# Low-rank outputs of a recurrence: two 64-row products on the two row halves of the array in place of two zero-padded 128-row products

## The chip, the core and the metric

The kernel runs on one core of a Trainium2 chip. The metric is the device time of one execution in microseconds (us), median of the runs. Engines are named as in the profile: PE is TensorE's matmul side, PEld its weight load, DVE VectorE, ACT ScalarE, POOL GpSimd, SP the engine that issues most of the DMAs.

## The reference, cut to what matters

The program is a whole network block (feed-forward, an RWKV-7 recurrence beside dilated attention, feed-forward) followed by two layers of another block. The change lies in the preparation of the recurrence. D_MODEL and RWKV_WIDTH are 1024, SEQ is 256, DECAY_LORA and AAA_LORA are 64, GATE_LORA is 160:

```python
p = token_shift(p, mu)
r, k, v, wd, ad, gd = _split_last(p, (RWKV_WIDTH, RWKV_WIDTH, RWKV_WIDTH,
                                      DECAY_LORA, AAA_LORA, GATE_LORA))
w = -jax.nn.softplus(-(w0 + jnp.tanh(wd) @ w2)) - 0.5     # w2: 64 x 1024
decay = jnp.exp(-jnp.exp(w))
a = jax.nn.sigmoid(a0 + ad @ a2)                          # a2: 64 x 1024
g = jax.nn.sigmoid(gd) @ g2                               # g2: 160 x 1024
```

`tanh(wd) @ w2` (decay) and `ad @ a2` (the in-context learning rate) contract over 64 rows each, the gate over 160.

## The kernel before, in words

Activations lie transposed: channels on the 128 partitions, the 256 tokens along the free dimension. Each of the 8 output tiles (KT = 8) of a projection to 1024 channels is one PSUM bank region of 128 x 256. All operands are float32, and every `matmul` of the source shows as two weight-load records and two MATMUL records in the trace ("x64" in a row is 32 matmuls). All matmuls of the kernel go through one helper, line 1055.

Each engine's program is written out by hand in its order, and semaphores join them: PE counts finished tiles up in `tile_done`, ACT counts the tiles that it has read out of PSUM up in `act_out`, and PE waits for `act_out` before it writes a bank again. Work is divided into stages, in this order around the change:

1. `rwkv_lora_in`: 3 tiles of 8 matmuls; ACT copies each tile (line 2348), DVE blends it with the token before (lines 3175, 3177) into the slot `sBH` of `arena`. Slot tile 0 then holds wd on partitions 0 to 63 and ad on 64 to 127, tile 1 the first 128 rows of gd, tile 2 its last 32 rows on partitions 0 to 31. DVE has zeroed tile 2 whole (line 3161) and the upper half of tile 3 (line 3160) ahead of that.
2. `rwkv_k`: 8 tiles of 8 matmuls. Beside its first tiles ACT prepares the low-rank inputs (lines 2355 to 2359): it copies ad to tile 3, takes tanh of wd, writes zeros over ad in tile 0, takes the sigmoid of gd, and says `lora_ready`.
3. `rwkv_lora_out` (lines 1382 to 1399 on PE, 2362 to 2376 on ACT): the stage of the change. For each of 8 channel tiles j there are three PSUM tiles, numbered q = 3j + c and written to bank q % 4: c = 0 decay, c = 1 learning rate, c = 2 gate. The weight slab has w2 on partitions 0 to 63 and a2 on 64 to 127 of its first part, so both products of before use all 128 rows of that part, against tile 0 (wd over zeros) and against tile 3 (zeros over ad). The gate takes two accumulated matmuls. ACT reads each tile out (lines 2371, 2373, 2375), and ahead of tile q = 9 it takes a square over the whole key tensor (line 2366). PE waits ahead of tile q until tile q - 4 has been read out.
4. `head_sums`: 4 matmuls of 512 columns to banks 4 to 7; then `rwkv_r0` and so on, projections of 8 matmuls per tile to banks 0 to 3.

Of the kernel before, what the change touches and what calls it, by code (L numbers as in the profile page):

```python
# [15 lines left out]
ACT = mybir.ActivationFunctionType  # L16
AX = mybir.AxisListType

P = 128
D = 1024  # L20
KT = D // P
T = 256
# [3 lines left out]
SLAB = 32 * P  # L26
# [509 lines left out]
def program(nc, x_in, ctx_in, wide_in, down_in, par_in, const_in, const1_in, const2_in, out, dbg=None):  # L536
    with ExitStack() as ctx:
# [15 lines left out]
        S = {n: ctx.enter_context(nc.semaphore(n)) for n in sem_names}  # L553

        def sb(name, n):
            return ctx.enter_context(nc.sbuf_tensor(name, [P, n], F32))

        ring = sb("weights", SLOTS * SLAB)
# [12 lines left out]
        bank = [ctx.enter_context(nc.psum_tensor(f"bank{b}", [P, 512], F32)) for b in range(8)]  # L571
# [8 lines left out]
        def tiles(buf, base, n, width):  # L580
            return buf[:, base:base + n * width].rearrange("p (k t) -> p k t", k=n)
# [28 lines left out]
        def wtile(st, j, q, n=P):  # L610
            base = st.slot(j) * SLAB + q * P
            return ring[:, base:base + n]


        def slot(k):
            return A[:, k * HALF:(k + 1) * HALF]

        def slot3(k):
            return slot(k).rearrange("p (k t) -> p k t", k=KT)

        sR, sA, sB, sK, sBH, sKH, sV, sL, sAA, sG = range(10)
# [282 lines left out]
        def rows_gi_em(n):  # L904
            return (ROWS_GI, ROWS_EM)[n]
# [43 lines left out]
        def fn_folded(g, ns):  # L949

            low = ZF[:, 2 * g, 0:ns]
            odd_sums = A[:, 14336 + g * 2 * EVEN:14336 + g * 2 * EVEN + ns * EVEN].rearrange("p (s t) -> p s t", s=ns)
            return low[:, :, 0:EVEN], odd_sums, low[:, :, EVEN:T]
# [96 lines left out]
        def _(pe):  # L1050
            t = Tally(pe, S, None)
            mm = nc.tensor.matmul

            def matmul(out, lhsT, rhs, start=True, stop=True):
                return mm(out, lhsT, rhs, start=start, stop=stop, skip_group_check=True)  # L1055

            def transpose(out, in_):
                return nc.tensor.transpose(out, in_, ident[0:in_.shape[0], 0:in_.shape[0]])  # L1058
# [323 lines left out]
            st = ST["rwkv_lora_out"]  # L1382
            arrived(st, 0)
            t.wait("lora_ready")
            lora = tiles(A, sBH * HALF, 4, T)
            for j in range(KT):
                for c in range(3):
                    q = 3 * j + c
                    pe.wait_ge(S["act_out"], st.act0 + q - 3)
                    cols = ring[:, st.slot(0) * SLAB:st.slot(0) * SLAB + 3 * D].rearrange("p (a n) -> p a n", a=3)[:, :, j * P:(j + 1) * P]  # L1390
                    dst = bank[q % 4][:, 0:T]
                    if c == 0:
                        last = matmul(dst, cols[:, 0], lora[:, 0])
                    elif c == 1:
                        last = matmul(dst, cols[:, 0], lora[:, 3])
                    else:
                        matmul(dst, cols[:, 1], lora[:, 1], stop=False)
                        last = matmul(dst, cols[:, 2], lora[:, 2], start=False)
                    last.then_inc(S["tile_done"], 1)

            def head_sums(ready, src, done):

# [282 lines left out]
            st = ST["dil_qk"]  # L1685
            arrived(st, 2)
            for c in range(4):
                for k in range(KT):
                    last = matmul(bank[c][:, 0:T], wtile(st, 2, c * KT + k), H1[:, k], start=k == 0, stop=k == KT - 1)
# [9 lines left out]
            for q in range(2):  # L1699
                for k in range(12):  # L1700
                    n = 24 * q + 2 * k
                    last = matmul(bank[4][:, n:n + 2], sq[:, k, q * P:(q + 1) * P], pair[:, 0:P:64])
# [5 lines left out]
            for k in range(6):  # L1708
                for q in range(2):
                    n = 24 * q + 12 + 2 * k  # L1710
                    cols = (k % 2) * T + q * P
                    for g in range(2):
                        rows = slice(64 * g, 64 * g + 64)
                        last = matmul(bank[5 + k // 2][rows, cols:cols + P], DIL_R[:, n + g:n + g + 1].to_broadcast([P, 64]), ident)
# [67 lines left out]
            for q in range(2):  # L1782
                for b in range(2):
                    for c in range(3):
                        last = transpose(bank[4 + 2 * q + b][:, c * P:(c + 1) * P], y1[:, q, (3 * b + c) * P:(3 * b + c + 1) * P])
# [32 lines left out]
            for la in range(2):  # L1818
                nq = 2 * T if la == 0 else T
                p = f"l{la}_"  # L1820
# [37 lines left out]
                for n in range(2):  # L1858
                    for c in range(4):
                        last = transpose(bank[5 + n][:, c * P:(c + 1) * P], rows_gi_em(n)[:, c * P:(c + 1) * P])  # L1860
# [173 lines left out]
                for g in range(4):  # L2034
                    out = bank[4][32 * g:32 * g + 32, 0:ns * EVEN].rearrange("p (s t) -> p s t", s=ns)
                    last = matmul(out, DFT_EDGE, fn_folded(g, ns)[0])
                last.then_inc(S["pe_for_act"], 1)
                t.wait("fn_halves", 4)
                if la == 0:
# [26 lines left out]
                    last = FT // 2 - 1  # L2066
# [13 lines left out]
                else:  # L2080
# [16 lines left out]
                    for which in BLOCKS:  # L2097
                        half, q = int(which[0]) - 1, int(which[1]) - 1
                        turn_out(which, lambda i: bank[X_BANKS[2 * half + i // 2]][:, (i % 2) * T + q * P:(i % 2) * T + (q + 1) * P])
            out_sq = tiles(G, 0, KT, T)  # L2100
            for k in range(KT):
                t.wait("squares_ready")
                for q in range(2):
                    last = matmul(bank[1][:, 2 * q:2 * q + 2], out_sq[:, k, q * P:(q + 1) * P], ones[:, 0:2], start=k == 0 and q == 0, stop=k == KT - 1)
            last.then_inc(S["sums_ready"], 1)
            t.wait("rstd_ready")
            for q in range(2):
                last = matmul(bank[5][:, q * P:(q + 1) * P], RSTD[:, 2 * q:2 * q + 1].to_broadcast([P, P]), ident)
# [4 lines left out]
        def _(act):  # L2113
            t = Tally(act, S, "act_steps")
            af = nc.scalar.activation
# [236 lines left out]
            shift_in("k", 0)  # L2352
            act.wait_ge(S["shift_done"], 3)
            lora = tiles(A, sBH * HALF, 4, T)
            t.step(af(lora[64:128, 3], lora[64:128, 0], ACT.Copy))
            t.step(af(lora[0:64, 0], lora[0:64, 0], ACT.Tanh))
            t.step(af(lora[64:128, 0], lora[64:128, 0], ACT.Copy, scale=0.0))
            t.step(af(lora[:, 1], lora[:, 1], ACT.Sigmoid))
            t.out(af(lora[0:32, 2], lora[0:32, 2], ACT.Sigmoid), "lora_ready")
            for q in range(1, 8):  # L2360
# [1 line left out]
            st = ST["rwkv_lora_out"]  # L2362
            for q in range(24):
# [3 lines left out]
                j, c = q // 3, q % 3  # L2367
# [132 lines left out]
            for b in range(4):  # L2500
                t.wait("dve_for_act")
                cols = slot(sV)[:, b * 512:(b + 1) * 512]
# [6 lines left out]
            for n in range(14):  # L2509
# [15 lines left out]
                for tile in dil_filled(n):  # L2525
                    if tile >= 4:
                        st = ST["dil_gate0"]
# [37 lines left out]
            for la in range(2):  # L2565
                nq = 2 * T if la == 0 else T
                qtiles = nq // P
                p = f"l{la}_"
# [144 lines left out]
                if la == 0:  # L2713
# [22 lines left out]
                    st = ST[p + "ffn_up"]  # L2736
# [64 lines left out]
        def _(dve):  # L2801
            t = Tally(dve, S, "dve_steps")
# [354 lines left out]
            for k in range(KT):  # L3157
                t.out(stt(H1[:, k], columns[k], pc("mix_norm", k), r, mul, mul), "h_ready")
            shift = H[:, HALF:HALF + 4 * 257].rearrange("p (b n) -> p b n", b=4)
            t.step(nc.vector.memset(slot3(sBH)[0:64, 3], 0.0))  # L3160
            t.step(nc.vector.memset(slot3(sBH)[:, 2], 0.0))
            t.out(nc.vector.memset(shift[:, :, 0:1], 0.0), "dve_for_act")
            dif = H[:, HALF + 1040:HALF + 1296]
            n_shift = [0]
# [95 lines left out]
            for b in range(4):  # L3260
                c = slice(b * 512, (b + 1) * 512)
# [267 lines left out]
            for la in range(2):  # L3529
                nq = 2 * T if la == 0 else T  # L3530
                qtiles = nq // P
                p = f"l{la}_"
# [200 lines left out]
                for n in range(len(units) + 3):  # L3733
# [4 lines left out]
                    if n >= 3:  # L3738
                        h, q = units[n - 3]
# [66 lines left out]
                if la == 0:  # L3806
# [35 lines left out]
                    st = ST[p + "ffn_up"]  # L3842
# [59 lines left out]
                else:  # L3902
                    fn_gates = tiles(A, 16384, 4, 2 * T)
                    merge(p + "fn", G2, nq, False, halves=(fn_gates, fn_gates))
                    for j in range(2):
                        st = ST[p + "out"]
# [25 lines left out]
            for half in range(2):  # L3932
                dve.wait_ge(S["x_gained"], 4 * half + 4)
                rows = slice(4 * half, 4 * half + 4)
# [260 lines left out]
```

## Time and profile before

| | |
|---|---|
| median of 3 runs | 3098.05 us (3097.92 to 3098.75) |
| the profiled execution | 3097.39 us, span 3095.6 us |
| PE busy | 3022.0 us, 98% of the span |
| DVE, ACT, POOL busy | 1705.4, 600.4, 520.0 us |
| the stage of the change on PE | 259.16 to 273.86 us of the span |
| mean granted TensorE clock | 0.993 of full speed |

The span runs from the first to the last instruction; a time of the trace is counted from the span's start. In rows of a timeline a piece merges neighbouring instructions of one kind: its second figure runs from the first start to the last end, and since a matmul is pipelined (its end lies well behind the moment at which the next can start), how long a group occupied PE is read from its start to the start of the next group. "128*128" or "64*128" is the part of the array that is used (rows * columns), "128x256" the moving operand (partitions x columns).

### The profile page before, as it was taken

What the parts mean: (1) busy time and instruction counts of PE and PEld (TensorE: products, weight loads), DVE (VectorE), ACT (ScalarE), POOL (GpSimd) and SP (SyncE); (2) the same over time, 40 slices, a digit from 0 to 9 for tenths busy, and PEclk for the clock granted to TensorE, in tenths of its full rate; (3) what the DMA queues carried; (4) which work ended last, traced back from release to release, by engine and by line L of the source; (5) the groups of instructions that cost most, each with busy time, mean ns of one, the idle gap of its engine ahead of it and who ended that gap; (6) DMA issues with size and microseconds to landing.
All of it is one profiled execution on the core that took longest, in us unless ns stands there. A gap on an engine that the chain in (4) does not pass through costs nothing.

```text
span 3095.6 us, 37908 instructions
## 1 busy us (share of the span) xinstructions
PE 3022.0 (98%) x15542; PEld 2275.2 (74%) x15542; DVE 1705.4 (55%) x2518; ACT 600.4 (19%) x1186; POOL 520.0 (17%) x210
## 2 busy tenths in 40 slices
PE   8999999999999999999999999999999999999999
PEld 4448788775448857887588888888888888678544
DVE  6744642547766556666863358777424513722574
ACT  2104212222111112102611121110021201511111
POOL 4320000013332100221021212221110001000332
PEclk9999999999999999999999999999999999999999
DMA  5544411345553311442012234443232143133452
GB/s 222 207 171 167 187 57 33 133 151 176 194 190 109 123 41 63 148 136 95 28 68 82 82 143 143 155 142 137 97 116 93 64 160 112 55 150 129 153 189 109
DMA packets 54812, 388.14 MB, mean 125 GB/s; under 512 B 8816, under 2 KB 23152, under 8 KB 33776
## 3 DMA queue, kind: packets, MB, share of 16 engines
q1 hardware_dynamic: 50000, 380.48, 34.2%
q10 hardware_dynamic: 4640, 5.24, 0.8%
q8 instruction: 123, 2.02, 0.3%
q14 instruction: 49, 0.40, 0.0%
HBM read 371.79 MB, written 1.05 MB: 120 GB/s over the span
## 4 chain that ended last, share of the span: by engine, by line
PE 92%; DVE 5%; ACT 1%; issue 1%; DMA 0%; DVEq 0%; SPq 0%; ACTq 0%
PE bank L1055 91%; PE bank L1058 1%; DVE factors L3074 0%; DVE factors L2976 0%; DVE weights L3061 0%; DVE h_T L2858 0%; DVE small L3720 0%; DVE arena L3091 0%; DVE weights L3064 0%; DVE masks L3853 0%; DMA params<-params_dram 0%; ACT arena L2676 0%; DVE arena L3764 0%; ACT h_T L2164 0%; DVE arena L3675 0%
## 5 line engine op out<-in xcount | busy, mean ns | idle before, releaser
L1055 PE MATMUL bank<-h_T,weights 128*128 128x256 f32 (+1 forms) x3184 | 779.5, 397 | 16.3 <-ACT h_T L2164 4.0
L1055 PEld LDWEIGHTS bank<-h_T,weights 128*128 128x128 f32 x3184 | 598.9, 191 | 156.0 <-issue 69.3
L2785 POOL TENSOR_TENSOR weights<-weights 128x1024 f32<-128x1024 f32 (+2 forms) x103 | 264.3, 2566 | 1337.2 <-DMA weights<-wide_slabs_dram 1238.7
L2796 POOL TENSOR_TENSOR factors<-weights 128x1024 f32<-128x1024 f32 (+2 forms) x103 | 257.7, 2502 | 1206.7 <-PE bank L1055 1022.3
L1055 PE MATMUL bank<-arena,weights 128*128 128x256 f32 x1784 | 397.0, 381 | 4.9 <-DVE arena L3466 2.5
L1055 PEld LDWEIGHTS bank<-arena,weights 128*128 128x128 f32 x1784 | 339.6, 191 | 54.2 <-DVE arena L3466 2.7
L1055 PE MATMUL bank<-weights,h_T 128*128 128x256 f32 (+2 forms) x1040 | 339.6, 475 | 3.5 <-DMA weights<-wide_slabs_dram 2.2
L1055 PE MATMUL bank<-factors,weights 128*128 128x256 f32 x1432 | 323.9, 379 | 5.9 <-DVE arena L3091 4.3
L1055 PE MATMUL bank<-weights,factors 128*128 128x256 f32 (+1 forms) x936 | 304.1, 470 | 2.7 <-DVE weights L3061 1.5
L1055 PEld LDWEIGHTS bank<-factors,weights 128*128 128x128 f32 x1432 | 271.7, 190 | 44.2 <-DVE arena L3091 5.5
L1055 PEld LDWEIGHTS bank<-weights,h_T 128*128 128x128 f32 x1040 | 198.0, 191 | 127.1 <-issue 101.7
L3061 DVE TENSOR_TENSOR weights<-weights,factors 128x1024 f32<-128x1024 f32 (+2 forms) x103 | 127.4, 1237 | 266.0 <-PE bank L1055 240.5
L1055 PEld LDWEIGHTS bank<-weights,factors 128*128 128x128 f32 x936 | 178.8, 192 | 112.4 <-issue 93.3
L3064 DVE TENSOR_TENSOR weights<-weights,factors 128x1024 f32<-128x1024 f32 (+2 forms) x103 | 130.7, 1269 | 169.7 <-PE bank L1055 168.6
L2274 ACT ACTIVATE arena<-bank 128x512 f32<-128x512 f32 (+1 forms) x144 | 83.3, 580 | 695.3 <-PE bank L1055 622.9
L1055 PE MATMUL bank<-factors 128*128 128x256 f32 (+3 forms) x808 | 214.4, 411 | 0.0
L3091 DVE TENSOR_TENSOR arena<-bank,arena 128x512 f32<-128x512 f32 (+1 forms) x132 | 88.1, 667 | 194.7 <-PE bank L1055 192.0
L1055 PEld LDWEIGHTS bank<-factors 128*128 128x128 f32 (+1 forms) x808 | 150.9, 190 | 48.8 <-issue 31.8
L1055 PE MATMUL bank<-arena 64*64 64x64 f32 (+7 forms) x1544 | 174.0, 304 | 9.7 <-ACT arena L2676 6.4
L1055 PE MATMUL bank<-weights,arena 128*128 128x512 f32 x396 | 174.5, 593 | 3.3 <-DVE weights L3061 3.3
L1055 PEld LDWEIGHTS bank<-arena 64*64 64x64 f32 (+2 forms) x1544 | 122.2, 160 | 52.1 <-issue 24.8
L3853 DVE SCALAR_TENSOR_TENSOR masks<-arena 128x1024 f32<-128x1024 f32 x88 | 152.5, 1733 | 2.9
(367 smaller groups left out, 2662.1 us busy)
## 6 DMA issues: line engine op xcount, KB each, us to landing
weights<-wide_slabs_dram SPq DMA_DIRECT2D x147, 2048.0 KB, 7.8
arena<-wide_slabs_dram SPq DMA_DIRECT2D x61, 512.0 KB, 4.1
weights<-down_slabs_dram SPq DMA_DIRECT2D x8, 1408.0 KB, 6.1
merged_T<-arena SPq DMA_DIRECT2D x240, 32.0 KB, 1.9
merged_T<-wide_slabs_dram SPq DMA_DIRECT2D x15, 512.0 KB, 4.6
arena<-arena ACTq DMA_DIRECT2D x16, 256.0 KB, 9.9
weights<-wide_slabs_dram SPq DMA_DIRECT2D x3, 1024.0 KB, 5.1
masks<-second_consts_dram SPq DMA_DIRECT2D x2, 1024.0 KB, 5.0
```

The costliest lines, as they stand in the source:

```text
L1055: return mm(out, lhsT, rhs, start=start, stop=stop, skip_group_check=True)
L1058: return nc.tensor.transpose(out, in_, ident[0:in_.shape[0], 0:in_.shape[0]])
L2274: af(place(u)[into], bank_of(u, of), ACT.Copy, scale=scale).then_inc(S["snapped"], 1)
L2785: nc.gpsimd.tensor_tensor(b[2], b[2], b[3], ALU.add).then_inc(S["first_sums"], 1)
L2796: nc.gpsimd.tensor_tensor(e, b[2], b[0], ALU.subtract).then_inc(S["first_sums"], 1)
L3061: ins = tt(b[0], b[3], e, sub)
L3064: ins = tt(b[1], b[1], e, sub)
L3091: ins = stt(dst, src, 1.0 / 16, dst, mul, add) if "ml_k" in u.name else tt(dst, src, dst, add)
L3853: ins = stt(ADA_PRODUCT, ada_tile(b), 1.0, COND_ROWS[:, s * D:(s + 1) * D], mul, mul, accum_out=ada_all[:, column:column + 1])
```

## The change

Decay and learning rate become two matmuls with 64 contraction rows each, the first on partitions 0 to 63 of weights and inputs, the second on 64 to 127, issued one behind the other to two banks with one wait for both. The last 32 rows of the gate become a matmul with 32 contraction rows. With nothing padded, the copy and the zeroing on ACT and the two memsets on DVE go. The built program has 16 matmuls on a 64 x 128 part of the array more than before (8 on the lower half of the rows, 8 on the upper), 8 on a 32 x 128 part, and 24 fewer on the whole array; the number of matmuls stays 7981.

```diff
             for j in range(KT):
-                for c in range(3):
-                    q = 3 * j + c
-                    pe.wait_ge(S["act_out"], st.act0 + q - 3)
-                    cols = ring[...].rearrange("p (a n) -> p a n", a=3)[:, :, j * P:(j + 1) * P]
-                    dst = bank[q % 4][:, 0:T]
-                    if c == 0:
-                        last = matmul(dst, cols[:, 0], lora[:, 0])
-                    elif c == 1:
-                        last = matmul(dst, cols[:, 0], lora[:, 3])
-                    else:
-                        matmul(dst, cols[:, 1], lora[:, 1], stop=False)
-                        last = matmul(dst, cols[:, 2], lora[:, 2], start=False)
-                    last.then_inc(S["tile_done"], 1)
+                cols = ring[...].rearrange("p (a n) -> p a n", a=3)[:, :, j * P:(j + 1) * P]
+                pe.wait_ge(S["act_out"], st.act0 + 3 * j - 2)
+                for c in range(2):
+                    rows = slice(64 * c, 64 * c + 64)
+                    matmul(bank[(3 * j + c) % 4][:, 0:T], cols[rows, 0], lora[rows, 0]).then_inc(S["tile_done"], 1)
+                q = 3 * j + 2
+                pe.wait_ge(S["act_out"], st.act0 + q - 3)
+                dst = bank[q % 4][:, 0:T]
+                matmul(dst, cols[:, 1], lora[:, 1], stop=False)
+                matmul(dst, cols[0:32, 2], lora[0:32, 2], start=False).then_inc(S["tile_done"], 1)
...
-            t.step(af(lora[64:128, 3], lora[64:128, 0], ACT.Copy))
             t.step(af(lora[0:64, 0], lora[0:64, 0], ACT.Tanh))
-            t.step(af(lora[64:128, 0], lora[64:128, 0], ACT.Copy, scale=0.0))
             t.step(af(lora[:, 1], lora[:, 1], ACT.Sigmoid))
             t.out(af(lora[0:32, 2], lora[0:32, 2], ACT.Sigmoid), "lora_ready")
...
-            t.step(nc.vector.memset(slot3(sBH)[0:64, 3], 0.0))
-            t.step(nc.vector.memset(slot3(sBH)[:, 2], 0.0))
```

On PE, at the start of `rwkv_lora_out` (`bank0` to `bank3` are PSUM banks, `arena` holds the low-rank inputs, `weights` the slab; a size is that of the output), before:

```order
L1055 MATMUL bank0<-arena,weights 128x256 [waits act_out,lora_ready,landed2]
L1055 MATMUL bank1<-arena,weights 128x256 [waits act_out]
L1055 MATMUL bank2<-arena,weights 128x256 [waits act_out]
L1055 MATMUL bank2<-arena,weights 128x256
L1055 MATMUL bank3<-arena,weights 128x256 [waits act_out]
L1055 MATMUL bank0<-arena,weights 128x256 [waits act_out]
L1055 MATMUL bank1<-arena,weights 128x256 [waits act_out]
L1055 MATMUL bank1<-arena,weights 128x256
```

and of the change:

```order
L1055 MATMUL bank0<-arena,weights 128x256 [waits act_out,lora_ready,landed2]
L1055 MATMUL bank1<-arena,weights 128x256
L1055 MATMUL bank2<-arena,weights 128x256 [waits act_out]
L1055 MATMUL bank2<-arena,weights 128x256
L1055 MATMUL bank3<-arena,weights 128x256 [waits act_out]
L1055 MATMUL bank0<-arena,weights 128x256
L1055 MATMUL bank1<-arena,weights 128x256 [waits act_out]
L1055 MATMUL bank1<-arena,weights 128x256
```

The order of the matmuls and their banks stay; the second of each three tiles has lost its wait, and the first waits for what the second waited for.

On ACT, in the preparation of the low-rank inputs between the copies of the tiles of `rwkv_k` (L2348), before:

```order
L2348 ACTIVATE h_T<-bank0 128x256 [waits tile_done]
L2355 ACTIVATE arena<-arena 64x256 [waits shift_done]
L2356 ACT_TABLE_LOAD
L2356 ACTIVATE arena<-arena 64x256 [waits act_steps]
L2357 ACTIVATE arena<-arena 64x256 [waits act_steps]
L2358 ACT_TABLE_LOAD
L2358 ACTIVATE arena<-arena 128x256 [waits act_steps]
L2359 ACTIVATE arena<-arena 32x256 [waits act_steps]
```

and of the change, whose lines stand three to five lower:

```order
L2345 ACTIVATE h_T<-bank0 128x256 [waits tile_done]
L2352 ACT_TABLE_LOAD
L2352 ACTIVATE arena<-arena 64x256 [waits shift_done]
L2353 ACT_TABLE_LOAD
L2353 ACTIVATE arena<-arena 128x256 [waits act_steps]
L2354 ACTIVATE arena<-arena 32x256 [waits act_steps]
```

Two activations are gone; both table loads stay.

## Rows read from the trace of the kernel before

**Rows 1.** The page, part 1: busy time, share and instructions of each engine.

```profile
PE 3022.0 (98%) x15542; PEld 2275.2 (74%) x15542; DVE 1705.4 (55%) x2518; ACT 600.4 (19%) x1186; POOL 520.0 (17%) x210
```

**Rows 2.** The chain that ended last, 215 to 300 us: start, us, what.

```profile
220.55 43.97 PE bank L1055 x200
...
264.54 0.38 ACT arena L2375
264.93 1.81 ACT arena L2366
...
266.76 0.48 ACT arena L2371
...
267.28 32.73 PE bank L1055 x149
```

**Rows 3.** Timeline of PE, 258 to 285 us: start, us, operation [idle before <-releaser].

```profile
259.16 7.50 PE L1055 MATMUL bank<-arena,weights 128*128 128x256 f32 x34
267.28 6.74 PE L1055 MATMUL bank<-arena,weights 128*128 128x256 f32 x30 [0.62 <-ACT arena L2371]
273.86 3.60 PE L1055 MATMUL bank<-arena,common 128*128 128x512 f32 x8
277.30 7.93 PE L1055 MATMUL bank<-h_T,weights 128*128 128x256 f32 x36
```

**Rows 4.** Timeline of all engines, 258 to 292 us: one row of ACT.

```profile
281.00 0.38 ACT L2348 ACTIVATE h_T<-bank 128x256 f32<-128x256 f32 x1 [1.01 <-PE bank L1055]
```

**Rows 5.** Timeline of PE, 2647.4 to 2652 us, the second layer's attention scores.

```profile
2647.45 1.13 PE L1055 MATMUL bank<-arena 64*128 64x512 f32 x4
2648.51 1.13 PE L1055 MATMUL bank<-h_T,weights 128*128 128x256 f32 x4
2649.57 1.13 PE L1055 MATMUL bank<-arena 64*128 64x512 f32 x4
2650.63 1.13 PE L1055 MATMUL bank<-h_T,weights 128*128 128x256 f32 x4
```

**Rows 6.** Timeline of PE, 1459 to 1472 us, the first layer's scores.

```profile
1463.86 0.70 PE L1055 MATMUL bank<-arena 64*128 64x256 f32 x4
1464.49 1.12 PE L1055 MATMUL bank<-h_T,weights 128*128 128x512 f32 x2
```

**Rows 7.** Lines of ACT, 259 to 274 us: xcount | busy, mean ns | idle before.

```profile
L2371 ACT ACTIVATE arena<-bank,params 128x256 f32<-128x256 f32 x8 | 3.8, 476 | 0.3
L2373 ACT ACTIVATE arena<-bank,params 128x256 f32<-128x256 f32 x8 | 3.8, 475 | 0.0
L2375 ACT ACTIVATE arena<-bank 128x256 f32<-128x256 f32 x7 | 2.7, 384 | 2.2 <-PE bank L1055 2.2
```

**Rows 8.** Timeline of all engines, 218 to 262 us: the removed work on DVE and ACT.

```profile
224.15 0.27 DVE L3160 MEMSET arena<- 64x256 f32 x1
224.54 0.27 DVE L3161 MEMSET arena<- 128x256 f32 x1
...
235.60 0.41 ACT L2355 ACTIVATE arena<-arena 64x256 f32<-64x256 f32 x1
...
237.77 0.41 ACT L2357 ACTIVATE arena<-arena 64x256 f32<-64x256 f32 x1
```

**Rows 9.** Windows: length, busy (count) of PE, PEld, DVE, ACT, POOL, granted clock, DMA share, GB/s.

```profile
259.00:276.00 17.00, 16.38 (x71) 13.15 (x70) 3.20 (x3) 13.43 (x27) 0.00 (x0) 1.00 0.42 139
...
2640.00:2698.00 58.00, 56.73 (x309) 38.15 (x307) 48.56 (x105) 34.78 (x80) 0.00 (x0) 1.00 0.12 41
...
918.00:921.40 3.40, 3.17 (x8) 2.57 (x9) 3.15 (x8) 3.31 (x8) 1.87 (x1) 0.50 0.50 212
921.40:925.00 3.60, 3.60 (x18) 3.19 (x17) 3.53 (x6) 0.93 (x2) 0.00 (x0) 1.00 0.00 0
```

More of the change, by code:

```diff
@@ L1386, in _ @@
             for j in range(KT):
-                for c in range(3):
-                    q = 3 * j + c
-                    pe.wait_ge(S["act_out"], st.act0 + q - 3)
-                    cols = ring[:, st.slot(0) * SLAB:st.slot(0) * SLAB + 3 * D].rearrange("p (a n) -> p a n", a=3)[:, :, j * P:(j + 1) * P]
-                    dst = bank[q % 4][:, 0:T]
-                    if c == 0:
-                        last = matmul(dst, cols[:, 0], lora[:, 0])
-                    elif c == 1:
-                        last = matmul(dst, cols[:, 0], lora[:, 3])
-                    else:
-                        matmul(dst, cols[:, 1], lora[:, 1], stop=False)
-                        last = matmul(dst, cols[:, 2], lora[:, 2], start=False)
-                    last.then_inc(S["tile_done"], 1)
+                cols = ring[:, st.slot(0) * SLAB:st.slot(0) * SLAB + 3 * D].rearrange("p (a n) -> p a n", a=3)[:, :, j * P:(j + 1) * P]
+                pe.wait_ge(S["act_out"], st.act0 + 3 * j - 2)
[7 more added lines that the diff above has]
+                matmul(dst, cols[0:32, 2], lora[0:32, 2], start=False).then_inc(S["tile_done"], 1)
             def head_sums(ready, src, done):
```

## Prediction

> **What bounds the kernel now.** I read the page's busy shares first, then the chain that ended last, then the timeline of the stage, then windows with the granted clock. PE is busy for 98% of the span [rows 1], so a stage is worth what it changes on PE, unless PE waits there. The chain around the change is PE from 220.55 us to the tile that ACT reads at 264.54, then ACT's square (line 2366), one more read of ACT, and PE again from 267.28 to 300 [rows 2]. So everything ahead of `rwkv_lora_out` (the inputs' preparation on ACT and DVE) lies beside PE work, and in the stage itself PE's own stream counts but for one stall, at the square. The stage holds 64 MATMUL records (34 + 30) and lasts from 259.16 to the head sums' start at 273.86: 14.70 us [rows 3]. A 512-column record takes (277.30 - 273.86) / 8 = 0.430 us [rows 3], one of 256 columns so 0.215; 64 of them are 13.76 us, and the other 0.94 us are the stall.
>
> **What goes off the path.** The two memsets (0.27 us each, 0.7 with their gaps) and the two activations (0.41 us each) [rows 8] end 20 us and more before PE needs `lora_ready` at 259.16; PE runs on `rwkv_k` meanwhile with no wait in the chain [rows 2]. ACT is free about 0.9 us sooner after the preparation, and no PE row waits for it. I take 0; an earlier copy of a tile cannot lengthen anything either, and a gain is excluded because PE has no idle time there to give back. No DMA is moved.
>
> **What two 64-row matmuls on the two halves cost.** The kernel already has this shape in its attention scores: two matmuls (four records), rows 0 to 63 and 64 to 127, to two banks. With 256 columns such a pair starts at 1463.86 and the next full-array work at 1464.49: 0.63 us [rows 6]. With 512 columns it is 2648.51 - 2647.45 = 1.06 us [rows 5]. One after the other, four records would be 0.86 and 1.72 us, so the two halves stream at the same time (two record times, 0.43 and 0.86), and 0.20 us comes on top in each case. The full-array block between two such pairs shows the same: four 256-column records between 2648.51 and 2649.57 last 1.06 us [rows 5] where 4 x 0.215 = 0.86, again 0.20 more. So the overlap is whole, and **each change of the array shape costs about 0.20 us**, in both directions: the next weights are not loaded ahead, they start together with the first matmul of the new shape.
>
> **The sum per channel tile j.** Before: 8 records x 0.215 = 1.72 us. After: the pair counts two record times, the gate's first matmul two, its second (32 rows) two: 6 x 0.215 = 1.29 us. And there are three changes of shape, 32 rows to 64, 64 to 128, 128 to 32: 0.60 us. Together 1.89 us. The overlap saves 0.43 us and the changes cost 0.60: every j gets 0.17 us longer. A 32-row shape is in no row of this kernel. From below its two changes cost nothing (if the chip kept 32 rows in the shape of its neighbour), from above I take twice the measured price, 0.40 each; I choose 0.20, since the change into and out of the 64-row shape cost that alike [rows 5].
>
> The Trainium skill bears on that choice: in "TensorEngine Tiling (Array Packing)", section Key Properties, it says that changing the tiling mode, and not just the tile, drains TensorE, and its list of configurations has 32 rows as a mode of its own. By it all three changes per j cost, and the sum is the one above; the 0.20 us of this trace [rows 5] fits a drain, but for 32 rows no row shows it yet. The same page's table "Theoretical Speedup" (up to 2x at 64 rows, up to 4x at 32) would promise the opposite if it were read per matmul: by it alone j would take 2 + 2 + 0.5 record times, 0.97 us. The trace agrees with the 2x only for two matmuls on different halves and only before the drains.
>
> **The stall.** Before, PE ends j = 2 at 259.16 + 3 x 1.72 = 264.32. ACT reads tile 8 at 264.54, squares, reads tile 9 at 266.76 [rows 2], and PE goes on at 267.28 [rows 3], 2.96 us after its end of j = 2. It waited with tile 13, since tile 12 needed only tile 8 read out. After, j = 2 ends at 259.16 + 3 x 1.89 = 264.83 and the release comes at 264.83 + 2.96 = 267.79. Now the one wait for the pair holds tile 12 back too, and behind it on PE stands everything else; but tile 12 streams beside tile 13 afterwards, so this costs no record of its own. PE is done with j = 3 at 259.16 + 4 x 1.89 = 266.72 and waits 1.07 us. One change of shape (32 to 64) is hidden in that wait.
>
> From 267.79: j = 4 takes 1.29 + 2 x 0.20 + 0.12 (the exposed first weight load, which before shows as 6.58 us for 30 records of 6.45 [rows 3]) = 1.81; j = 5 to 7 take 3 x 1.89 = 5.67; the change back to the full array takes 0.20. The head sums start at 275.47 instead of 273.86: **+1.6 us**. ACT keeps up: its three reads per j are 476, 475 and 384 ns [rows 7], 1.34 us against 1.89. Nothing of it is hidden behind the stage either: after the head sums PE goes straight on [rows 3], and ACT waits for PE there again (1.01 us, at 281.00) [rows 4]. So the delay goes through to the end: span 3095.6 + 1.6 = 3097.2, that execution 3097.39 + 1.6 = 3099.0. The median of the runs lies 0.66 us above the profiled execution, and from it I get 3098.05 + 1.6 = 3099.6 us. That is 0.05%; this kernel's measurement can tell about 0.2% (6.2 us) from no change, so by that bound it is the same.
>
> **Rivals.**
> 1. *The 32-row matmul keeps the neighbour's shape*, two changes per j (128 to 64 and back). P = 1.69; the release comes at 259.16 + 5.07 + 2.96 = 267.19, then 1.29 + 0.20 + 0.12 + 3 x 1.69 = 6.68: head sums at 273.87, +0.0 us, 3098.1. For it: no row has 32 rows. Against: each shape change that the trace has does cost.
> 2. *The changes cost nothing here*, the gain that the overlap alone would give. P = 1.29: release at 265.99, then 4 x 1.29 + 0.12: head sums at 271.27, -2.6 us, 3095.5. Against: all four intervals between shapes that the rows hold, three in [rows 5] and one in [rows 6], have 0.20 in them.
> 3. *Changes beside 32 rows cost double*: P = 1.29 + 0.20 + 0.40 + 0.40 = 2.29; the release comes at 268.99 and the rest takes 2.01 + 6.87 + 0.40: head sums at 278.27, +4.4 us, 3102.5.
> 4. *Slower by over 0.2%: the clock falls in the stage.* Half the rows idle and PE waiting at every drain, the granted clock drops from 2.4 to 1.2 GHz at its start and stays there. A record then takes 0.43 us, j takes 6 x 0.43 + 0.60 = 3.18, which swallows the stall, and the stage 8 x 3.18 + 0.20 = 25.6 instead of 14.7: +10.9 us, 3109. It decides from a clock of 0.50 over more than half of the stage. Against: the score stages, with the same pairs and changes in them, have 1.00 from 2640 to 2698, as this stage has now [rows 9].
> 5. *A half-clock stretch elsewhere comes or goes*, as work shifts by 1.6 us. The trace has such stretches behind pauses, as at 918.00: 8 records in 3.40 us at 0.50, 18 in 3.60 right after at 1.00 [rows 9]. So one more or one less of that length is worth about 1.7 us either way: 3097.9 or 3101.3.
>
> **How the numbers follow.** Forecast 0.58; rivals 1 to 5: 0.12, 0.05, 0.07, 0.03, 0.15. The range runs from 3096.6 (nearly rival 1 with a stretch less, 3096.4) to 3102.4 (nearly rival 3); rival 2 below and rival 4 above are left out with part of rival 3, together under 0.15. Only rival 4 is beyond 0.2%, and no case gains so much: with every change of shape free it is still only -2.6. Faster 0.01, same 0.95, slower 0.04 (with 0.01 for a cause that I do not see).
>
> **What the profile after would show.** The pair's records of one j starting within hundredths of each other, 0.43 us per pair; between the first records of neighbouring blocks 0.63 us each, three blocks per j, 1.89 in all; every block's weight load starting with its matmul. ACT's square near 265.3 and PE idle ahead of tile 12 (0.8 to 1.1 us); the head sums near 275.5. If the gate's two blocks merge into 0.86 us, rival 1 holds; if the head sums start before 273, rival 2; a clock under 1.00 between 259 and 276 is rival 4. The forecast is wrong if the head sums start before 274.5 or after 276.5, or if the end moves otherwise than they do.

## The result, and the profile after

| | us |
|---|---|
| forecast | 3099.6 (3096.6 to 3102.4) |
| changed kernel, median of 15 runs | 3104.59 (3097.71 to 3109.79) |
| kernel before, median of 15 runs, same session | 3098.26 (3096.72 to 3101.97) |
| ratio | 1.0018, 95% interval 1.0011 to 1.0025 |
| profiled execution of the changed kernel | 3100.48, span 3098.7 |

The changed kernel is slower, by 0.11 to 0.25%; whether that is more than the 0.2% that the prediction took as its bound, the interval leaves open. The median lies 2.2 us above the forecast's range. The profiled execution is one of the quicker ones (fourth of 15) and shows only the part that was forecast. Three things of the spread matter: it is 12 us wide, against 5 us before; it is also wider for the kernel before than the three runs shown first; and among the 15 runs the time follows the mean granted clock (3097.71 us at 0.994, 3109.79 at 0.989).

The page after, part 1, answers to [rows 1]:

```profile
PE 3026.2 (98%) x15542; PEld 2270.2 (73%) x15542; DVE 1703.7 (55%) x2516; ACT 598.9 (19%) x1184; POOL 523.1 (17%) x210
```

Timeline of PE in the changed kernel, answering to [rows 3] (a merged piece carries the shape of its first record):

```profile
259.32 7.61 PE L1055 MATMUL bank<-arena,weights 64*128 64x256 f32 x32
267.83 7.61 PE L1055 MATMUL bank<-arena,weights 64*128 64x256 f32 x32 [0.89 <-ACT arena L2366]
275.37 3.70 PE L1055 MATMUL bank<-arena,common 128*128 128x512 f32 x8
278.91 8.37 PE L1055 MATMUL bank<-h_T,weights 128*128 128x256 f32 x38
```

PE was restarted at 267.83 (forecast 267.79) and the head sums began at 275.37 (forecast 275.47). The two agree better than the terms behind them: the stage began 0.16 us late, at 259.32, and took 16.05 us, where the forecast had 16.31. Timeline of all engines, the weight loads alone: each block's loads come in one piece at its start.

```profile
259.32 0.30 PEld L1055 LDWEIGHTS bank<-arena,weights 64*128 64x128 f32 x4 [0.33 <-issue]
...
259.95 0.30 PEld L1055 LDWEIGHTS bank<-arena,weights 128*128 128x128 f32 x2 [0.33 <-ACT h_T L2345]
...
260.58 0.29 PEld L1055 LDWEIGHTS bank<-arena,weights 32*128 32x128 f32 x2 [0.33 <-issue]
...
261.20 0.30 PEld L1055 LDWEIGHTS bank<-arena,weights 64*128 64x128 f32 x4 [0.33 <-ACT arena L2368]
```

From 259.32 to 259.95 the pair, to 260.58 the gate's 128-row matmul, to 261.20 its 32-row one: 0.63, 0.63 and 0.62 us, three changes of shape per channel tile. A change into or out of the 32-row shape costs as much as one of the 64-row shape. Below, "drain" is short for such a change and its 0.20 us. ("ACT" behind the arrow is only what ended last before the load; the 0.33 us stand also where no ACT is named.) The chain, answering to [rows 2], and the windows, to [rows 9]:

```profile
265.08 0.38 ACT arena L2370
265.47 1.81 ACT arena L2361
...
267.30 0.48 ACT arena L2366
...
267.83 32.29 PE bank L1055 x144
```

```profile
259.00:268.00 9.00, 8.11 (x36) 3.74 (x36) 3.20 (x3) 6.55 (x13) 0.00 (x0) 1.00 0.64 233
268.00:276.00 8.00, 8.00 (x34) 3.78 (x35) 0.00 (x0) 5.42 (x15) 0.00 (x0) 1.00 0.00 0
```

The removed work on ACT let the copy of the next key tile start at 239.57 instead of 240.39, and nothing came of it, as forecast. The span is 3.1 us longer than before. From the stage's start to `rwkv_r0`'s it is 19.59 us against 18.14, so 1.5 us are the change's. The rest lies elsewhere; half-clock stretches came and went there, which were not added up one by one. One of them is in this window of the changed kernel, which has a clock of 1.00 in the profile before:

```profile
1838.00:1848.00 10.00, 9.36 (x53) 6.04 (x51) 1.75 (x5) 2.07 (x4) 1.29 (x1) 0.66 0.87 301
```

So this execution explains 1.5 us by the change, not the 6.3 between the medians.

### The profile page after: what moved, and what is told of

Its sections match the earlier page's. It is cut to its first block, busy times and chain, and to the rows that moved or that the text cites. A ratio compares the mean times of both kernels' runs of the same rounds, so it can differ in the third digit from the quotient of the medians.

```text
span 3098.7 us, 37904 instructions
## 1 busy us (share of the span) xinstructions
PE 3026.2 (98%) x15542; PEld 2270.2 (73%) x15542; DVE 1703.7 (55%) x2516; ACT 598.9 (19%) x1184; POOL 523.1 (17%) x210
## 4 chain that ended last, share of the span: by engine, by line
PE 92%; DVE 5%; ACT 1%; issue 1%; DMA 0%; DVEq 0%; SPq 0%; ACTq 0%
PE bank L1055 91%; PE bank L1058 1%; DVE factors L3069 0%; DVE factors L2971 0%; DVE weights L3056 0%; DVE h_T L2853 0%; DVE small L3713 0%; DVE arena L3086 0%; DVE weights L3059 0%; DVE masks L3846 0%; DMA params<-params_dram 0%; DVE arena L3757 0%; DVE arena L3668 0%; DVE small L3650 0%; ACT arena L2671 0%
## 5 line engine op out<-in xcount | busy, mean ns | idle before, releaser
L1055 PE MATMUL bank<-arena,weights 128*128 128x256 f32 (+1 forms) x1784 | 397.0, 382 | 5.1 <-DVE arena L3459 2.5
L1055 PEld LDWEIGHTS bank<-arena,weights 128*128 128x128 f32 (+1 forms) x1784 | 334.0, 190 | 60.2 <-issue 4.8
```

## The experiments

**E1, the changed kernel again** (no edit).

> The changed kernel a second time. What is open: its stage is 1.5 us longer in the trace, its median 6.3 us. Theory H (the clock falls within the new stage in many executions, since PE is fed less densely there: drains at every change of shape, half-used rows and a wait of about 1 us): a spread of some 10 us again, the time following the mean granted clock of the execution, median 3104 +- 2; a profile of a slow execution shows 0.50 between 264 and 280 us. Rival S (half-clock stretches elsewhere come and go with the phase of the work, as in the kernel before): the median is nearer to 3100, and a profile shows the stage at 1.00 and the added half-clock stretches elsewhere.

Median 3105.66 us (3097.0 to 3109.83, 11 runs), ratio 1.0011 (1.0000 to 1.0022); four runs lie between 3097.0 and 3098.3, seven between 3103.2 and 3109.8, none in the gap (the first 15 runs have no such gap). The median of the kernel before in the same session was 3100.45 us. This time the profiled execution was one of the long ones (span 3107.1 us). Its PE timeline:

```profile
260.45 7.61 PE L1055 MATMUL bank<-arena,weights 64*128 64x256 f32 x32
268.95 13.80 PE L1055 MATMUL bank<-arena,weights 64*128 64x256 f32 x32 [0.89 <-ACT arena L2366]
282.69 5.40 PE L1055 MATMUL bank<-arena,common 128*128 128x512 f32 x8
287.92 12.25 PE L1055 MATMUL bank<-h_T,weights 128*128 128x256 f32 x56
```

and its windows (length, busy and count of PE, PEld, DVE, ACT, POOL, granted clock, DMA share, GB/s):

```profile
260.00:269.00 9.00, 8.11 (x37) 3.72 (x35) 3.20 (x3) 6.42 (x13) 0.00 (x0) 1.00 0.65 233
269.10:275.00 5.90, 5.90 (x15) 2.65 (x16) 0.00 (x0) 2.50 (x7) 0.00 (x0) 0.50 0.00 0
275.00:286.10 11.10, 11.10 (x22) 4.64 (x22) 0.00 (x0) 4.11 (x8) 0.00 (x0) 0.50 0.23 61
286.10:300.00 13.90, 13.90 (x61) 11.40 (x60) 7.46 (x12) 3.54 (x7) 0.00 (x0) 1.00 0.25 104
```

Up to the wait the stage is the same to 0.01 us (8.50 against 8.51 from its start to PE's restart). Right after PE's wait at the square the clock fell from 2.4 to 1.2 GHz and stayed there through the rest of the stage and 3.4 us of head sums. The second half took 13.74 us instead of 7.54. From the stage's start to `rwkv_r0`'s: 27.47 us here, 19.59 in the profile above. One such fall costs 7.9 us. At half clock a channel tile takes 13.74 / 4 = 3.44 us. Rival 4 had 3.18, since it left a change of shape at 0.20 us; with six record times of 0.43 the change comes to about 0.29 us there.

**E2, the same delay without the change.**

```diff
+            for n in range(3):
+                matmul(bank[4][:, 0:T], pair, lora[:, 1])
+            matmul(bank[4][:, 0:P // 2], pair, lora[:, 1, 0:P // 2])
+            matmul(bank[4][:, 0:P // 2], pair, lora[:, 1, 0:P // 2])
             head_sums("act_for_pe", slot3(sKH), "pe_for_act")
```

> The kernel before with five matmuls more ahead of the head sums (into a bank that those overwrite): six records of 256 columns and four of 64, 1.5 to 1.7 us of dense work on the whole array. It delays all that follows as the change does and leaves the stage dense. Theory H: 1.5 to 1.7 us above the kernel before and as narrow a spread. Rival S (the delay itself sets the clock loose elsewhere): about 5 to 6 us above and the wide spread of the changed kernel.

3099.13 us (3097.29 to 3101.73, 11 runs), ratio 0.9995 (0.9987 to 1.0004). In the trace the added work is there: 19.88 us from the stage's start to `rwkv_r0`'s, 1.7 more than before. In the times it does not show; the interval reaches to +1.2 us, so the 1.5 to 1.7 us that Theory H expected were missed as well. But the 5 to 6 us of the rival lie far outside: the delay does not by itself shake loose half-clock stretches elsewhere that would be worth that much.

**E3 and E4, the stage twelve times over**, before and changed:

```diff
-    add("rwkv_lora_out", 1, 24, 24, 0)
+    add("rwkv_lora_out", 1, 288, 288, 0)
...
-            for j in range(KT):
+            for n in range(12 * KT):
+                j = n % KT
...
-            for q in range(24):
+            for q in range(288):
```

> The kernel before with the low-rank output stage done twelve times over (same operands, same results, the square each time). A repeat costs 14.7 us as in the profile, 11 of them 162 us: about 3260 us, granted clock 1.00 in all twelve by theory H and by rival S.

> The changed kernel with its stage done twelve times over. At full clock a repeat is 8 x 1.89 us and 1.07 us of wait, 16.1 us: 11 of them 177 us, about 3276 to 3282 us. Rival S: that, and a clock of 1.00 in all twelve. Theory H: the clock is 0.50 in some or most of the repeats, each of which then takes up to 25.4 us; the total is 3290 to 3380 us.

E3: 3261.43 us (4 runs), 14.70 us a repeat. E4: 3413.51 us (3409.95 to 3421.09, 4 runs), above even the 3290 to 3380 of Theory H. PE timeline of E3, two of its twelve stalls, and the windows of E4:

```profile
267.36 14.08 PE L1055 MATMUL bank<-arena,weights 128*128 128x256 f32 x64 [0.62 <-ACT arena L2377]
282.06 14.08 PE L1055 MATMUL bank<-arena,weights 128*128 128x256 f32 x64 [0.62 <-ACT arena L2377]
```

```profile
259.00:269.70 10.70, 9.81 (x44) 4.48 (x42) 3.20 (x3) 7.79 (x16) 0.00 (x0) 1.00 0.55 196
269.70:420.00 150.30, 150.30 (x351) 65.48 (x350) 0.00 (x0) 62.52 (x137) 0.00 (x0) 0.50 0.00 0
420.00:587.00 167.00, 167.00 (x384) 72.57 (x383) 0.00 (x0) 70.08 (x150) 0.00 (x0) 0.50 0.01 4
587.00:600.00 13.00, 13.00 (x56) 10.42 (x55) 6.40 (x10) 3.54 (x7) 0.00 (x0) 0.99 0.28 120
```

In E4's profile the clock falls 2 us after the first wait's end (267.79) and does not rise in eleven more repeats, though PE no longer waits for ACT at that speed. The timeline has the stage's end at 583.88 us, 314 us later; the clock is back some 3 us into the full-array head sums. The 316 us from the first wait's end are 11.5 repeats of 27.5 us each, which is 8 x 3.44; the expectation had at most 25.4, with drains priced as at full clock, and that is why the total lies above its range. E3 has a wait in every repeat too, of 0.62 us, and its twelve stalls come evenly 14.70 us apart at a clock of 1.00. So the stage can let the clock fall, and in this profile the mix of shapes did not raise it again.

**E5, the pairs alone** (the gate's last part zero-padded on the whole array again, with its memset):

```diff
-                matmul(dst, cols[0:32, 2], lora[0:32, 2], start=False).then_inc(S["tile_done"], 1)
+                matmul(dst, cols[:, 2], lora[:, 2], start=False).then_inc(S["tile_done"], 1)
```

> Half of the change: the 64-row pairs stay, the gate's last 32 rows are again a matmul on the whole array against a zeroed tile. Two changes of shape per channel tile, 1.69 us each; by the sum at full clock the head sums start at 273.9 us of the span, as before. Theory H64 (the 64-row pairs and their drains are what lets the clock fall): wide spread, median 3 us or more above the kernel before. Theory H32 (the 32-row matmul, which keeps a quarter of the rows busy, is what does it): same as the kernel before within 0.5 us, and no wider spread than that.

3098.75 us (3094.94 to 3102.46, 11 runs), ratio 0.9996 (0.9987 to 1.0005). The head sums start 14.61 us after the stage (259.33 to 273.94), 14.70 before. That is rival 1's sum (+0.0), for the kernel that it describes: the overlap (0.43 us) about pays for two drains (0.40 us). The profiled execution has a clock of 1.00 in the stage, and none of the 11 runs is above 3102.46 us.

**E9, the 32-row gate part alone** (decay and learning rate padded as before):

```diff
-                        last = matmul(dst, cols[:, 2], lora[:, 2], start=False)
+                        last = matmul(dst, cols[0:32, 2], lora[0:32, 2], start=False)
```

> The other half of the change: decay and learning rate zero-padded on the whole array as before, the gate's last part a 32-row matmul. Two changes of shape per channel tile, 8 x 0.215 + 2 x 0.20 = 2.12 us; PE hardly waits at the square; the head sums start at 276.6 us, 2.8 us later than before, at full clock. Theory H32: wide spread and 6 us or more above the kernel before. Theory H64: 2.8 us above, narrow.

3101.1 us (3096.99 to 3105.19, 11 runs), ratio 1.0004 (0.9995 to 1.0013). The head sums start at 276.60 us, where the expectation put them, but the stage began late, at 259.48: it takes 17.12 us, 2.4 longer than before and not 2.8, and PE hardly stands still in it. The median is 1.5 us above that of the kernel before in the same session, within the interval. The profiled execution (3103.28 us) has a clock of 1.00 in the stage. The highest of the 11, 3105.19 us, has no trace, so a fall in it is not excluded.

**E10 and E11, each half twelve times over.**

> Twelve times the stage with pairs alone (gate zero-padded). At full clock 8 x 1.69 + 1.27 us of wait = 14.8 us a repeat, about 3262 us in all and clock 1.00. H64: long stretches at 0.50 as in the twelvefold changed stage (over 3330 us). H32: none.

> Twelve times the stage with the 32-row gate part alone. At full clock some 17.2 us a repeat, about 3290 us. H32: long stretches at 0.50, over 3350 us. H64: none.

3263.17 and 3295.46 us, one run each. Windows of E10, and of E11:

```profile
259.00:350.00 91.00, 84.49 (x399) 48.37 (x399) 3.20 (x3) 70.53 (x155) 0.00 (x0) 1.00 0.07 24
350.00:435.00 85.00, 78.49 (x369) 45.17 (x370) 0.00 (x0) 66.62 (x145) 0.00 (x0) 1.00 0.00 0
```

```profile
259.00:360.00 101.00, 100.81 (x379) 63.08 (x377) 3.20 (x3) 68.86 (x147) 0.00 (x0) 1.00 0.06 21
360.00:466.00 106.00, 105.80 (x395) 65.72 (x394) 0.00 (x0) 72.33 (x155) 0.00 (x0) 1.00 0.00 1
```

Neither half alone does it, in twelve repeats of one execution each, not even the pairs with a wait of 1.08 us in every repeat, which is longer than the 0.89 us of the changed kernel. Neither H64 nor H32 holds.

**E7 and E12, the changed stage without PE's wait**: its tiles go over all eight banks, so PE runs on through ACT's square. Once, and twelve times over.

```diff
-                pe.wait_ge(S["act_out"], st.act0 + 3 * j - 2)
+                pe.wait_ge(S["act_out"], st.act0 + 3 * j - 6)
...
-                    matmul(bank[(3 * j + c) % 4][:, 0:T], cols[rows, 0], lora[rows, 0])...
+                    matmul(bank[(3 * j + c + 4) % 8][:, 0:T], cols[rows, 0], lora[rows, 0])...
...
-                pe.wait_ge(S["act_out"], st.act0 + q - 3)
+                pe.wait_ge(S["act_out"], st.act0 + q - 7)
...
+            pe.wait_ge(S["act_out"], st.act0 + 20)
             head_sums("act_for_pe", slot3(sKH), "pe_for_act")
```

> The changed kernel with the same eight banks: PE's wait of 1 us at ACT's square goes, all changes of shape stay; 15.3 us at full clock, 0.6 more than the kernel before's stage. Theory W (it takes the wait on top of the drains to let the clock fall): 1 us above the kernel before at most, narrow. Rival (the drains and part-filled rows alone do it): wide spread and 3 us or more above, as the changed kernel.

> Twelve times the changed stage over eight banks, without PE's wait at the square. Full clock: 15.1 us a repeat, about 3265 us. Theory W: clock 1.00. Rival (drains alone): 0.50 for hundreds of us as in the twelvefold changed stage, 3400 us.

E7: 3099.58 us (3095.82 to 3102.51, 11 runs), ratio 1.0000 (0.9991 to 1.0009). The stage takes 15.09 us (260.41 to 275.50), and no execution is above 3102.51 us, where seven of E1's eleven were above 3103.2. E12: 3261.66 us, one run, 24 changes of shape in each repeat. Its windows:

```profile
259.00:350.00 91.00, 91.00 (x389) 42.99 (x387) 3.21 (x3) 67.44 (x150) 0.00 (x0) 1.00 0.07 24
350.00:440.00 90.00, 90.00 (x384) 42.66 (x384) 0.00 (x0) 67.29 (x150) 0.00 (x0) 1.00 0.00 0
```

With the same matmuls, in the same shapes and order, the clock holds over twelve repeats once PE does not wait. Set beside E4's 314 us at half clock and E7's eleven runs, this says that the fall takes the wait on top of the drains. Three things stay open in that. E12 is one execution. E4 and E12 ran on different chips; on E12's chip the changed kernel fell in two of four executions (E13 to E16 below), but on E7's chip it was never run. And the edit takes the wait away by using other banks and so also packs PE's work closer: whether it takes the pause itself, or only the sum of the time that pause and drains leave PE without work, these runs do not tell apart.

**E6, the kernel before over eight banks** (the edit of E7, applied to the kernel before).

> The kernel before with this stage's tiles over all eight banks (bank (q + 4) % 8) and PE waiting for the tile eight before, not four, so that it runs on through ACT's square: 13.8 us instead of 14.7, 0.9 us faster in the trace; dense work, clock 1.00 by every theory.

3098.4 us (3095.23 to 3100.72, 11 runs), ratio 0.9998 (0.9990 to 1.0007). The stage is 13.81 us long (260.41 to 274.22), 0.9 shorter as forecast; the median moved 1.3 us the right way, within its interval.

**E8, a version for use**: the pairs of two channel tiles, then their four gate matmuls padded on the whole array, over eight banks.

```diff
+            W = 2
+            for j0 in range(0, KT, W):
+                for i in range(3 * W):
+                    q = 3 * j0 + i
+                    j, c = (j0 + i // 2, i % 2) if i < 2 * W else (j0 + i - 2 * W, 2)
...
+                    pe.wait_ge(S["act_out"], st.act0 + q - 7)
+                    dst = bank[(q + 4) % 8][:, 0:T]
```

> A version for use: the pairs of two channel tiles one behind the other, then the four gate matmuls of both on the whole array (zero-padded), over eight banks. Two changes of shape per two channel tiles: 2 x 0.43 + 0.20 + 4 x 0.43 + 0.20 = 2.98 us, four times 11.9 us, against 14.7: 2.8 us faster in the trace. If the clock falls in it (half of the rule of H64), the median is above the kernel before instead.

3095.93 us (3092.73 to 3100.41, 11 runs), ratio 0.9991 (0.9982 to 0.9999). PE timeline and window:

```profile
259.40 12.02 PE L1055 MATMUL bank<-arena,weights 64*128 64x256 f32 x64
271.26 3.60 PE L1055 MATMUL bank<-arena,common 128*128 128x512 f32 x8
```

```profile
259.00:276.00 17.00, 17.00 (x82) 11.43 (x81) 3.21 (x3) 13.22 (x29) 0.00 (x0) 1.00 0.56 196
```

The stage takes 11.86 us, 2.8 less than before, as summed. By the interval this version beats the kernel before by 0.01 to 0.18%; the changed kernel's medians, of other sessions, are 3104.59 and 3105.66 us. The gain has two parts. The eight banks give the 0.9 us that E6 shows. The other 1.9 are the forecast's own arithmetic with 8 changes of shape and all pairs kept: 8 x 0.43 us saved, 8 x 0.20 paid.

**E13 to E16, four more profiled executions of the changed kernel.**

> The changed kernel, one profiled execution. Theory H: where the clock falls to 0.50 at the stage's second half, the time is 3102 to 3110 us; where it stays at 1.00 there, 3097 to 3101 us. Rival: no such link.

> The changed kernel once more, same expectations: a fall at the stage's second half goes with 3102 to 3110 us, none with 3097 to 3101 us.

> The changed kernel once more, same expectations: a fall at the stage's second half goes with 3102 to 3110 us, none with 3097 to 3101 us.

> The changed kernel once more, same expectations: a fall at the stage's second half goes with 3102 to 3110 us, none with 3097 to 3101 us.

3099.71, 3108.19, 3102.89 and 3099.79 us. Windows from 268 to 276 us of E13, E14, E15 and E16, in this order:

```profile
268.00:276.00 8.00, 7.11 (x32) 3.37 (x31) 0.00 (x0) 5.83 (x15) 0.00 (x0) 1.00 0.00 0
```

```profile
268.00:276.00 8.00, 7.88 (x20) 3.51 (x20) 0.00 (x0) 3.16 (x9) 0.00 (x0) 0.50 0.00 0
```

```profile
268.00:276.00 8.00, 8.00 (x23) 3.61 (x24) 0.00 (x0) 3.75 (x10) 0.00 (x0) 0.60 0.00 0
```

```profile
268.00:276.00 8.00, 8.00 (x34) 3.78 (x34) 0.00 (x0) 5.43 (x15) 0.00 (x0) 1.00 0.00 0
```

With the first profile and E1's, six executions: three without the fall (3100.48, 3099.71, 3099.79 us), three with it (E1's and 3108.19, 3102.89). Of E15's PE timeline, the stage's start and `rwkv_r0`'s:

```profile
259.39 7.61 PE L1055 MATMUL bank<-arena,weights 64*128 64x256 f32 x32
...
285.27 13.98 PE L1055 MATMUL bank<-h_T,weights 128*128 128x256 f32 x64
```

These 25.88 us are 6.3 more than the 19.59 without a fall; in E1 and E14 it is 7.9 and 7.8. The fall does not always come at the wait's end: in E1 and E14 it does, in E15 and E4 1.7 and 2.0 us later.

How often it happens can only be estimated where there is no trace. Of the changed kernel's 30 executions (15, 11 and 4), 20 took over 3102 us, but so did 13 of the 85 executions of the kernel before; 15 of the 30 took longer than the longest of those 85 (3104.47 us). So the share is between a half and two thirds. By two thirds of 7.3 us, 4.9, and the 1.5 us of longer stage, the means should differ by 6.4 us, by one half 5.2; those of the first session differ by 5.7 (3104.49 against 3098.75), those of E1 by 3.5. The sizes fit, and no better than that.

## Why the prediction was wrong

**Right.** Most terms of the stage's sum: the pair's whole overlap (0.43 us saved), 0.20 us for a change of shape in every direction (0.63, 0.63 and 0.62 a block), 32 rows as a shape of its own, the wait moved ahead of tile 12, the restart at 267.83 and the head sums at 275.37. Two terms were a little off: the 0.12 us for an exposed first weight load did not come (four channel tiles after the wait took 7.54 us, where the forecast has 7.68 with the last change), and the wait ended 8.51 us after the stage's start, not 8.63. That the stage began 0.16 us late hid most of it, which is luck. The three profiled executions without a fall lie near the forecast of 3099.6: 3099.7, 3099.8 and 3100.5. Four of E1 lie 1 to 3 us below it, so the spread of the rest of the kernel is part of that agreement. Moving work off ACT and DVE was worth nothing. Rivals 1 to 3 are out for this kernel; rival 1's sum came true for the version that it describes, E5.

The Trainium skill's "TensorEngine Tiling (Array Packing)", section Key Properties, was the better guide for 32 rows: a change of tiling mode drains, and the trace agrees, at 0.2 us. The up to 2x of its section Theoretical Speedup is seen in the trace for two matmuls on different halves (0.43 us for four records, before the drain); the up to 4x for 32 rows is not seen for a 32-row matmul on its own, which takes 0.42 us as on 128 rows.

**Wrong: rival 4, the clock, dismissed at 0.03.** The step that failed reads: "Against: the score stages, with the same pairs and changes in them, have 1.00 from 2640 to 2698, as this stage has now [rows 9]." It took two stages, each with a part of what the new stage combines, for proof about the combination. The score stages have pairs and drains, but four full-array records between any two pairs [rows 5] and no 32-row matmul; which of these keeps their clock up was not tried. The stage before has the wait, but no drains. E10 (pairs and wait), E11 (32 rows, hardly a wait) and E12 (everything but the wait) each keep 1.00; only all together, in E4 and in part of the executions of the change, let it fall. Rival 4 was also drawn as all or nothing: half clock from the stage's start in every execution, +10.9 us. Measured is a fall at the wait or up to 2 us behind it, half-way through the stage, in three of six profiled executions and by the times in a half to two thirds of all, at 6.3 to 7.9 us each. It was also priced too low: a channel tile at half clock takes 3.44 us, not 3.18, and the half clock reached 3 us into the head sums, which rival 4 left out. As the median of runs decides, a fall in over half of them is all it takes.

Rival 5, stretches elsewhere, exists as spread (the runs of the kernel before range from 3095.5 to 3104.5 over all sessions, not 3097.9 to 3098.8), but in E2 the delay alone raised the median by 1.2 us at most. The prediction took each rival as one fixed time: between rival 3 at 3102.5 and rival 4 at 3109 it had nothing, and that is where the medians lie.

**Not settled.** Whether the wait has to be as long as 0.9 us, and which of the two shapes could be missing with a longer wait, was not tried. Why one execution falls and the next does not is not shown either: up to the wait the six have a clock of 1.00 from 200 us on, apart from a half-clock stretch near 221 us in E1 and E13, of which one fell and one did not.

## What to carry to other kernels

Price a change of array shape, not only the matmul: here 0.20 us each, so that a pair of 256-column float32 matmuls on the two row halves (0.43 us saved) breaks even at two changes and loses at three; put matmuls of one shape together (E8) and leave a lone 32-row product padded (E9: eight of them on their own made the stage 2.4 us longer). Where drains leave PE thinly fed, a wait that was harmless before can cost much more than its length: here the clock fell at it and came back only in full-array work. Remove the wait (more banks; worth 0.9 us even without drains, E6) before adding drains. When a profile explains a quarter of a median's shift, look at the spread and profile the kernel again before believing either.

## What the runs showed of the hardware that was not expected

- The granted clock fell to 0.50 at a PE wait of 0.9 us amid drains, or up to 2 us behind it, in three of six profiled executions, and not in twelve repeats with pairs and a wait of 1.1 us (E10), nor in twelve with the same matmuls and no wait (E12).
- Once at 0.50, a PE with no idle time in 314 us of 32-, 64- and 128-row matmuls stayed there (E4); it returned some 3 us into full-array work of 512 columns.
- A change of shape costs about 0.20 us at full clock and about 0.29 at half clock (E1, E4).
- A 32-row matmul of 256 columns takes about 0.42 us, as a 128-row one does, and its change of shape 0.20, as the 64-row one's. This was forecast, but no row of before showed it.
